# Column sums of the adaptive weights placed behind the third group of a round in two MLP stages

## The reference

```python
def sqrelu_mlp(x, w_up, w_down):
    return jnp.square(jax.nn.relu(x @ w_up)) @ w_down
```

## Time and profile before

| | |
|---|---|
| median of 3 runs | 2101.21 us (2100.18 to 2105.09) |
| profiled execution, its own time | 2098.89 us |
| span of the profiled execution | 2097.2 us |
| TensorE busy | 1957.3 us (93%) |
| VectorE busy | 1188.9 us (57%) |
| ScalarE busy | 776.5 us (37%) |
| GpSimd busy | 571.4 us (27%) |
| mean granted share of TensorE's clock | 0.961 |

### The profile page before, as it was taken

How to read it: one execution, slowest core, us unless ns; L and a number is a source line. 1 busy time by engine, 2 the same in 40 slices (tenths; PEclk the granted TensorE clock), 3 DMA queues, 4 the chain that set the end, 5 groups by cost and what they waited for, 6 DMA issues and landing times.

```text
span 2097.2 us, 25922 instructions
## 1 busy us (share of the span) xinstructions
PE 1957.3 (93%) x9708; PEld 1590.1 (76%) x9708; DVE 1188.9 (57%) x1998; ACT 776.5 (37%) x1314; POOL 571.4 (27%) x428
## 2 busy tenths in 40 slices
PE   7988889899999999998899999999999879999997
PEld 6875658778887888766787887878747777888875
DVE  4437576662464452285763266363448768777775
ACT  3236452331232142383332233354324263444432
POOL 2112351200000020181300001043241446777730
PEclk9999699999999999999999999999998989999998
DMA  6322002552353222202343255211120212333343
GB/s 214 110 83 81 1 7 98 196 191 91 111 190 120 81 101 97 85 2 100 139 162 121 101 180 184 101 61 61 61 80 1 101 63 98 121 121 110 111 148 133
DMA packets 38952, 221.11 MB, mean 105 GB/s; under 512 B 5888, under 2 KB 6336, under 8 KB 18368
## 3 DMA queue, kind: packets, MB, share of 16 engines
q1 hardware_dynamic: 27184, 177.89, 23.4%
q0 software_dynamic: 11664, 41.80, 6.1%
HBM read 215.55 MB, written 2.10 MB: 104 GB/s over the span
## 4 chain that ended last, share of the span: by engine, by line
PE 77%; DVE 13%; DMA 3%; POOL 2%; ACT 2%; issue 1%; SPq 1%; POOLq 0%; ACTq 0%; DVEq 0%
PE G L407 36%; PE G L2319 6%; PE G L2228 5%; PE TR L2319 4%; PE OB L2319 4%; PE G L1509 3%; PE G L2249 2%; PE TR L407 2%; POOL weights_low L430 1%; PE OB L407 1%; PE TR L1509 1%; PE OB L1509 1%; PE OB L1468 1%; PE TR L2228 1%; PE OB L2228 1%
## 5 line engine op out<-in xcount | busy, mean ns | idle before, releaser
L407 PE MATMUL G<-xt_high,weights_high 128*128 128x512 f32 (+2 forms) x1288 | 478.2, 371 | 19.4 <-POOL xt_low L1225 5.8
L424 ACT ACTIVATE weights_high<-ring_sb 128x1024 fp32r<-128x1024 f32 (+1 forms) x312 | 322.5, 1037 | 437.6 <-PE OB L2319 151.1
L430 DVE TENSOR_TENSOR weights_low<-ring_sb,weights_high 128x1024 fp32r<-128x1024 f32 x204 | 249.7, 1227 | 411.5 <-ACT weights_high L424 403.2
L407 PE MATMUL G<-xt_low,weights_high 128*128 128x512 f32 (+2 forms) x1288 | 474.8, 369 | 0.0
L407 PE MATMUL G<-xt_high,weights_low 128*128 128x512 f32 (+2 forms) x1288 | 474.7, 369 | 0.0
L430 POOL TENSOR_TENSOR weights_low<-ring_sb,weights_high 128x1024 fp32r<-128x1024 f32 (+1 forms) x108 | 267.5, 2490 | 402.9 <-ACT weights_high L424 349.1
L407 PEld LDWEIGHTS G<-xt_high,weights_high 128*128 128x128 f32 (+1 forms) x1288 | 243.5, 189 | 62.2 <-issue 18.1
L407 PEld LDWEIGHTS G<-xt_high,weights_low 128*128 128x128 f32 (+1 forms) x1288 | 243.2, 189 | 40.5
L407 PEld LDWEIGHTS G<-xt_low,weights_high 128*128 128x128 f32 (+1 forms) x1288 | 243.4, 189 | 39.7
L2114 POOL DMA_DIRECT2D KS_sb<-ada x64 | 33.8, 528 | 501.6 <-DVE og_sb L2663 501.6
L1967 DVE SCALAR_TENSOR_TENSOR KS_sb<-G,cols_sb,KS_sb 128x441 f32<-128x441 f32 (+2 forms) x176 | 121.1, 688 | 73.7 <-ACT KS_sb L1723 73.7
(11 more groups left out here) (470 smaller groups left out, 3637.1 us busy)
## 6 DMA issues: line engine op xcount, KB each, us to landing
ring_sb<-chunks SPq DMA_DIRECT2D x156, 1024.0 KB, 4.8
KS_sb<-ada POOLq DMA_DIRECT2D x64, 512.0 KB, 4.3
ring_sb<-slabs SPq DMA_DIRECT2D x3, 2048.0 KB, 7.8
X_sb<-x SPq DMA_DIRECT2D x4, 512.0 KB, 5.5
rows_sb<-ln_gain POOLq DMA_DIRECT2D x4, 512.0 KB, 5.1
rows_sb<-ln_bias POOLq DMA_DIRECT2D x4, 512.0 KB, 5.8
out<-X_sb SPq DMA_DIRECT2D x4, 512.0 KB, 4.9
table_sb<-table SPq DMA_DIRECT2D x1, 1146.0 KB, 15.8
```

The lines of the kernel that those rows point to most:

```text
L407: mm = nc.tensor.matmul(out, lhsT=a, rhs=b, start=(3 * i + j == 0), stop=(3 * i + j == n - 1))
L424: nc.scalar.activation(Wh[:, n % 4, c], raw_quarter(Q)[:, c], ACT.Copy).then_inc(w_hi, 1)
L430: tt_(out=Wl[:, n % 4, c], in0=raw_quarter(Q)[:, c], in1=Wh[:, n % 4, c], op=ALU.subtract).then_inc(w_lo, 1)
```

## The change

On TensorE the sum of a round goes behind its third up quarter (m = 2) instead of its fourth. The sum of part 0's round 0, which stood ahead of round 1, goes behind round 1's first quarter; round 1 of part 0 is written out for that. On VectorE a round's eight steps go behind groups 0 and 1, four each; in part 0's round 0 (`late`) 0, 2, 3 and 3 go behind groups 0 to 3. The move of a round's sum goes behind the same round's group 3; that of part 0's round 0 goes into round 1, behind the subtraction of group 0. VectorE's four rounds of a part are written out. The programs of GpSimd, ScalarE and SP stay as they are.

```diff
--- before.py
+++ after.py
@@ -2281,16 +2281,26 @@
                 for part, (up, down) in enumerate(PARTS[stage]):
                     if part:
                         pe.wait_ge(dve_out, v + 4)
+                    def up_quarter(i, m):
+
+                        pe.wait_ge(w_lo, i * 4 + (Q + m + 1))
+                        pe.wait_ge(act_out, i * 4 + (a + m - 3))
+                        w = [x[:, m, :].rearrange("p (k c) -> p k c", k=KT) for x in (Wh, Wl)]
+                        split_products(G[m][:, :], [(w[0][:, k, :], w[1][:, k, :], XTh[:, k, :], XTl[:, k, :])
+                                                    for k in range(KT)]).then_inc(quarters, 1)
+
+                    def four(i):
+                        for m in range(4):
+                            up_quarter(i, m)
+                            if m == 0 and part == 0 and isinstance(i, int) and i == 1:
+                                ada_sums(ada, 0)
+                            if m == 2:
+                                ada_sums(ada + part, i)
+
                     if part == 0:
-                        ada_sums(ada, 0)
-                    with pe.Fori(0 if part else 1, up // 4) as i:
-                        for m in range(4):
-                            pe.wait_ge(w_lo, i * 4 + (Q + m + 1))
-                            pe.wait_ge(act_out, i * 4 + (a + m - 3))
-                            w = [x[:, m, :].rearrange("p (k c) -> p k c", k=KT) for x in (Wh, Wl)]
-                            split_products(G[m][:, :], [(w[0][:, k, :], w[1][:, k, :], XTh[:, k, :], XTl[:, k, :])
-                                                        for k in range(KT)]).then_inc(quarters, 1)
-                        ada_sums(ada + part, i)
+                        four(1)
+                    with pe.Fori(0 if part else 2, up // 4) as i:
+                        four(i)
                     Q, a = Q + up, a + up
 
                     pe.wait_ge(ada_moved, 4 * (ada + part) + 4)
@@ -2708,8 +2718,8 @@
                 q, h = st(stage, "quarters"), st(stage, "hidden")
 
                 def four(part, i):
-                    if not (isinstance(i, int) and i == 0):
-                        ada_move(part, i, 1)
+                    late = n == 0 and i == 0
+                    steps = ((), (0, 1), (2, 3, 4), (5, 6, 7)) if late else ((0, 1, 2, 3), (4, 5, 6, 7), (), ())
                     for m in range(4):
                         if not (isinstance(i, int) and i == 0 and n == 0 and m == 0):
                             low_split(dve, nc.vector.tensor_tensor, stage, n + m + 3, i)
@@ -2720,15 +2730,16 @@
                         at = bass.ds(i * 4 + m, 1) if not isinstance(i, int) else slice(4 * i + m, 4 * i + m + 1)
                         nc.vector.tensor_tensor(out=Hl[:, at, :], in0=r.unsqueeze(1), in1=Hh[:, at, :],
                                                 op=ALU.subtract).then_inc(hidden, 1)
-                        ada_steps_of(part, i, ((0, 1, 2), (3, 4, 5), (6, 7), ())[m])
+                        if n == 0 and i == 1 and m == 0:
+                            ada_move(part, 0)
+                        ada_steps_of(part, i, steps[m])
+                        if m == 3 and not late:
+                            ada_move(part, i)
 
                 for part, (up, down) in enumerate(PARTS[stage]):
-                    four(ada + part, 0)
-                    with dve.Fori(1, 3) as i:
+                    for i in range(4):
                         four(ada + part, i)
-                    four(ada + part, 3)
                     n, u = n + up, u + up
-                    ada_move(ada + part, 3)
                     def add(half, t, scale):
                         nc.vector.scalar_tensor_tensor(out=X[:, t, half * 512:(half + 1) * 512], in0=X[:, t, half * 512:(half + 1) * 512],
                                                        scalar=scale, in1=BANKS[1 - half if part else half][t][:, :],
```

## The result

The changed kernel takes **2147.81 us** (median of four runs, 2141.84 to 2149.01) against 2101.28 before: 1.0212 times as long, 95% interval 1.0200 to 1.0225. The side was right and the size was not: 2117 was predicted, and 2147.81 lies outside the range of 2100 to 2136. The profiled execution took 2141.84 us, the quickest of the four, and is 42.95 us above the profiled execution of before.

What follows compares the result with a forecast made beforehand. TensorE, busy 93% of the span, was taken as the bound, through its idle time and 1.2 GHz stretches. +20.0 + 3.8 - 8.0 = +15.8 us on 2098.89 gave 2114.7; with 2.3 us to the median, 2117 us, range 2100 to 2136.

Steps and rivals of the forecast that it cites:

- Edit 1: Fourteen sums behind the third group: each stalls TensorE by 1.2 us, or 1.6 us in POOL's loop; +20.0 us.
- I take 4.4, nearer the lone row: Fourth weight load of a round: assumed to land in 4.4 us, between 4.1 (alone) and 5.5 us (overlapped).
- The upper row: Profile row of a load issued with others in flight, landing 5.5 us from its issue.
- POOL has only these loads in its queue: Claim that on POOL nothing else queues up behind the waits for the adaptive weight loads; no cost charged.
- Rival A: Fourth load lands before step 6 wants it, only VectorE's 0.5 us per sum remain: +2.8, 2104 us; chance 0.18.
- rival C: Clock falls behind the third groups too, 1.7 us for each of fourteen sums: 2141 us, 2129 from half; chance 0.11.
- one gap of 1.76 us: Lone idle gap in the attention, behind which the granted clock share stayed 1.00.
- Edit 2: At four parts' ends the sum no longer runs inside the wait for the move: 4 x 0.95 = +3.8 us.
- Edit 3: First sum of each MLP behind quarter 0 of round 1: idle 2.9 us, slow clock charged again; net -8.0 us.
- Edit 4: Loops written out: VectorE loses 0.12 us of register work per group, TensorE streams alike; zero.

Runs made afterwards that it cites:

- one-step loads: The changed kernel with the adaptive weights in eight loads of 256 KB into four buffers, instead of four of 512 KB into two: 2111.76 us, ratio 1.0054.

## Why the prediction was wrong

**Edit 1, the sum behind the third group: the mechanism held, and two sizes failed.** VectorE's part was forecast as 0.5 us per sum and is 0.77 (one-step loads). Four steps had been counted as 3.0 us and take 3.31 in one piece. **The step that failed first is "I take 4.4, nearer the lone row"** for the fourth load: it lands in 5.0 to 5.3 us in ten of the fourteen rounds, and the third, forecast to land in 4.1, in 3.9 to 4.3 in these rounds. With 0.7 us more the forecast waits of 1.2 outside GpSimd's loop and 1.6 inside it become 1.9 and 2.3; in the ten rounds they are 1.80 to 2.05 and 2.25 to 2.35, and 29.8 us in all for the 20.0 of the sum. The upper row, 5.5 us, had been the nearer one. The reason given for 4.4, "the neighbour's data are mostly across by then", was wrong: at the fourth load's issue the third had moved 0.07 of 0.52 MB. That no weight chunk moves at that time was right in the round shown above. That this overlap is why the fourth load takes 5.2 us is likely by these figures, but wasn't tried by itself. "POOL has only these loads in its queue" fails in the last round, where the layer norm's two loads stand behind the fourth (6.8 us, a wait of 3.60). The Trainium skill's fixed 2 us plus bytes over 436 GB/s ("DMA: Bandwidth & Descriptors", section "Anatomy of one DMA — SWDGE (gpsimd) path"), an estimate of 3.2 us for such a load, was under every landing of these loads in the MLPs of the changed kernel too (3.9 us and more). Rival A, which it supported, fell.

**The second failure is the clock, which the sum had at zero inside the rounds.** It fell behind nine of fourteen sums, 15 us. The prediction had it as rival C with a chance of 0.11, at 2129 us for half of the falls and 2141 for all, and gave it so little on the strength of one gap of 1.76 us without a fall. That gap stood alone; each of these waits is followed by a sum of another 1 us. So C's mechanism came true beside the longer waits, and neither alone gives the measured time. The two errors go together in the traces, one of each kernel: no fall behind 0.77 us of waiting, four in fourteen behind 1.5, nine in fourteen behind 2.1 on the mean. The range had been built from one error at a time, 35 us of waits or the clock, so that its upper end lay beneath their sum.

**Edit 2, the parts' ends: right.** The wait for the move grew from 2.19 to 2.97 and from 2.27 to 3.05 us, 9.0 to 12.1 in all, and the run with the last sums behind the fourth group has 9.0 again. With the sum's 1.05 us on the path, 0.95 + 2.19 us have become 1.05 + 2.97, 0.88 more at each end: 3.5 us for the forecast 3.8.

**Edit 3, the start: right in sign, 5.4 us for 8.0.** The wait of 2.9 us was met in the first MLP (2.67) and missed in the second (4.79). The forecast had counted 0.65 us of waiting for the third load and nothing for the fourth. In the second MLP VectorE waits for both, and the fourth lands 6.3 us from its issue at 1060.31:

```profile
1060.83 0.75 DVE L2673 SCALAR_TENSOR_TENSOR og_sb<-KS_sb,csil_sb,og_sb 128x512 f32<-128x512 f32 x1 [0.81 <-DMA KS_sb<-ada]
...
1066.59 1.54 DVE L2673 SCALAR_TENSOR_TENSOR og_sb<-KS_sb,csil_sb,og_sb 128x512 f32<-128x512 f32 x2 [1.89 <-DMA KS_sb<-ada]
```

**Edit 4, loops written out: nothing that shows.** No run has them alone; the two runs that keep them with the new start are 5 us faster than before.

The terms, corrected from the two traces: 29.8 of waits + 15.3 of clock (nine by 1.7) + 3.5 at the parts' ends + 1.0 for the ten other sums, which take 1.05 us instead of 0.95, - 6.2 at the start (its waits went from 12.8 to 7.5 us, and the first sum from 1.87 to 1.05) = 43.4 us. The two MLPs, each from its first square to the first down product of its last part, are 22.0 and 22.8 us longer, 44.8 together; the rest of the program happens to be 1.8 us shorter in that execution, so the spans differ by 43.0. The typical run of the changed kernel is 6 us longer than its profiled one, and no trace shows where. The mean granted clock was 0.959 in the profiled execution and 0.956 to 0.958 in the other three; 0.002 of 2147 us is an estimate of 4 us, which points to more falls, but that isn't shown.

## What to carry to other kernels

When an instruction of the bounding engine is moved forward in its program, ask how long its operands have been ready at the new place, not only whether they can be: here a sum that never waited was set 5.4 us earlier, just in front of data that come 0.6 to 3.6 us later. Behind such a wait price the clock as well, and widen the range by both together. And look where an instruction that somebody waits for stands in its own engine's program: moving `ada_move` over a square and a subtraction gained twice what the start gained.

## What the runs showed of the hardware

The clock's fall doesn't follow from the length of the wait alone. In one trace it fell behind a wait of 1.28 us (the sum at 1133.11, with a mean share of 0.63 in the 3.6 us behind it) and not behind one of 2.35 (at 1108.88, shown above):

```profile
1133.11 1.05 PE L2266 MATMUL OB<-ones_sb,og_sb 128*128 128x1 f32 x8 [1.28 <-DVE og_sb L2673]
```

```profile
1134.36:1137.96 3.60, 3.60 (x12) 2.89 (x11) 2.26 (x3) 0.00 (x0) 0.00 (x0) 0.63 0.89 253
```

Two DMA loads of 512 KB issued 1.65 us apart landed in 4.0 and 5.2 us, where a lone one took 4.1. The first had moved 0.07 MB when the second was issued.
